# Weight halves stored even columns first, read by TensorE as pairs 2 KB apart

## The chip, the cores and the metric

The kernel runs on one core of a Trainium2 chip. The metric is the device time of one execution in microseconds (us). The core has TensorE (PE, its weight loads are shown apart as PEld), VectorE (DVE), ScalarE (ACT), GpSimd (POOL) and SyncE (SP), which issues the loads.

## The reference

Two transformer-like blocks run one after the other on 256 tokens of width 2048, in float32. Cut to the matmuls, which matter here:

```python
# first block
h = rmsnorm(x);  proj = h @ w_in                 # 2048 -> 8192
y = concat(hgrn2_mixer(...), short_conv_mixer(...))   # mixer: small per-head products
x = x + y @ w_out
g, u = split(rmsnorm(x) @ w_gate_up);  x = x + (silu(g) * u) @ w_down
x = rmsnorm(x)
# second block
ada = silu(c) @ w_ada + b_ada                     # a vector times 2048 x 12288
proj = (rms(x) * (1 + sc1) + sh1) @ w_in          # 2048 -> 8256
y_a = mla_attention(...);  y_b = stick_breaking(...)  # 8 heads each, 256 tokens
x = x + gt1 * ((sig(gl_a) * (y_a @ w_mla) + sig(gl_b) * (y_b @ w_sb)) @ w_out)
g, u = split((rms(x) * (1 + sc2) + sh2) @ w_ffn_in);  x = x + gt2 * ((silu(g) * u) @ w_ffn_out)
```

With 256 tokens every weight is used once, and all of them (some 580 MB in float32) are streamed from device memory.

## The kernel before

A weight matrix comes in units of 512 rows by 512 columns: 1 MB, in SBUF as `raw` [128 partitions, 4, 512], one transfer each, four buffers in turn. A unit is worked in two chunks of two 128-row slices (`kt`). Float32 accuracy is had by splitting: for each chunk ACT casts `raw` to the rounded format float32r, `whi` [128, 2, 512] (L870 in `cast`), and DVE takes `wlo = raw - whi` (L1262 in `low`). The activations lie split in the same way, as stationary operands (`hH`/`hL`, `mH`/`mL`, `aH`/`aL` and others).

`products(v)` in `tensor_program` does a visit: for each of the two slices and each of the two halves of the tokens (`m`) three matmuls of 128 x 128 stationary by 512 moving columns into one PSUM bank: activation high by weight high (L839), high by low (L840), low by high (L841). So a chunk has 12 of them, each reading 512 adjacent float32r columns of `whi` or `wlo`. One block, `kpe`, has its weights as the stationary operand instead (L821 to L823, 48 matmuls of 256 columns).

The order is written out in `Plan`: blocks, chunks, visits, and for each visit which chunk is split then, three chunks ahead of its use (four buffers of `whi` and `wlo`, four more at two boundaries between stages). Between the visits stand the small pieces of the mixers, the attention, the norms and the transposes (L553), each under a semaphore. `w_ada` is multiplied on DVE from its own `raw` units (L1689). Some of the small pieces read their operands through patterns with steps. The one that the prediction uses is `pair_ap`, with which `hgrn` reads `Qx` as the moving operand of L633 on TensorE (plain float32; 8 matmuls a level, each shown as 2 passes of 128 columns) and `Kx` in the copies L1056 and L1061 on ACT:

```python
        def pair_ap(t, base, n, h):                                  # L502
            ap = t[:, :, :]
            return bass.AP(tensor=ap.tensor, offset=ap.offset + base,
                           ap=[list(ap.ap[0]), [2 * h, n // (2 * h)], [1024 + h, 2], [1, h]])
```

It reads `h` neighbours, then `h` neighbours 1024 + h elements on, and so by turns. The first level has h = 1: single elements, 4100 bytes apart. It doubles from level to level, up to 64. On DVE `carry` (L1667) goes through the same tensors in runs of h out of 2h elements, for h = 1 single elements at a step of 2, and L1635 reads both its inputs at a step of 2 elements; L1615 has its inputs in order.

Of the kernel before, what the change touches and what calls it, by code (L numbers as in the profile page):

```python
# [15 lines left out]
ALU = mybir.AluOpType  # L16
# [6 lines left out]
RAW = 4  # L23
# [233 lines left out]
class Counts:  # L257
# [13 lines left out]
    def ev(self, name, *key):  # L271
        self.n[name] = self.n.get(name, 0) + 1
        if not self.real:
            assert (name,) + key not in self.value, (name, key)
            self.value[(name,) + key] = self.n[name]
        return self.of(name), 1

    def on(self, name, *key):
        if not self.real:
            return self.of(name), 1  # L280
        return self.of(name), self.value[(name,) + key]
# [5 lines left out]
def two_block_kernel(nc, a, out):  # L287
    ctx = ExitStack()
    with ctx:
# [6 lines left out]
        ev, on = bk.ev, bk.on  # L296
# [11 lines left out]
        def take(n):  # L308
            o = top[0]
            top[0] += n + (-n) % 64  # L310
            return o

        def new(name, shape, dt=F32):
            return at(name, shape, dt, take(nbytes(shape)))

        raw = [new(f"raw{i}", [P, 4, 512]) for i in range(RAW)]
        whi = [new(f"whi{i}", [P, 2, 512], F32R) for i in range(HL)]
        wlo = [new(f"wlo{i}", [P, 2, 512], F32R) for i in range(HL)]
# [11 lines left out]
        kpe = new("kpe", [P, 2, 64])  # L330
# [5 lines left out]
        for i in range(7):  # L336
            o = take(2 * KB)
# [74 lines left out]
        def visit(v):  # L412

            return sem_visit, v + 1

        def acc(b, m):

            return banks[2 * (b.index % 2) + m]
# [25 lines left out]
        def side_read(*key):  # L444

            n = bk.bank.get(key, 0) if not bk.real else bk.bank[key]
            return sem_side[n % 4], n // 4 + 1

        def raw_here(u):

            return sem_raw[u % RAW], 16 * (u // RAW + 1)
# [38 lines left out]
        def f(ap):  # L490
            return ap.bitcast(F32)
# [10 lines left out]
        def pair_ap(t, base, n, h):  # L502
            ap = t[:, :, :]
            return bass.AP(tensor=ap.tensor, offset=ap.offset + base,
                           ap=[list(ap.ap[0]), [2 * h, n // (2 * h)], [1024 + h, 2], [1, h]])

        def ev_tmp(b, m):
            return T[2 * (b.index % 2) + m]

# [41 lines left out]
        def tensor_program(e):  # L551
# [3 lines left out]
            def turn_tokens(b, m, key):  # L555

                t, o = ev_tmp(b, m), next_bank(e, *key)
                for k in range(4):
                    ins = turn(o[:, P * k:P * k + P], t[:, P * k:P * k + P])
                ins.then_inc(*ev("pe_turn", *key))  # L560
# [201 lines left out]
            def amid(v):  # L762

                for w, v0 in enumerate(SK):
                    k = v - v0
                    if k == 7:
                        norm_first(w, 0, 2)
                        norm_first(w, 0, 3)
                    elif k in (11, 12):
                        norm_first(w, 1, 2 * (k - 11))  # L770
                        norm_first(w, 1, 2 * (k - 11) + 1)
                    elif 14 <= k <= 17:
                        norm_rest(w, 2 + (k - 14) // 2, (k - 14) % 2)

            def left_here(b, i, ci, m):
# [28 lines left out]
                elif b.kind == "out2" and b.arg == (0,) and i == 0 and m == 0 and kt % 4 == 0:  # L804
                    e.wait_ge(*side_read(pl.at["sb", kt // 4].index, 0))
                    e.wait_ge(*side_read(pl.at["sb", kt // 4].index, 1))

            def products(v):
                c, ms, _ = pl.visits[v]
                b, ci, u, hf = pl.chunks[c]  # L810
                wh, wl, (xh, xl) = whi[pl.buf[c]], wlo[pl.buf[c]], halves[b.lhs]
                if ms[0] == 0:
                    e.wait_ge(*on("dve_lo", c, 0))
                if b.kind == "kpe":
                    wh = wh[:, :, :].rearrange("p a b -> p (a b)").rearrange("p (k n) -> p k n", k=KT)
                    wl = wl[:, :, :].rearrange("p a b -> p (a b)").rearrange("p (k n) -> p k n", k=KT)
                    o = acc(b, 0)[0:64, 0:S]
                    if pl.acc_n[b.index, 0]:
                        e.wait_ge(sem_acc[2 * (b.index % 2)], pl.acc_n[b.index, 0])
                    for kt in range(KT):  # L820
                        e.matmul(o, wh[:, kt, :], xh[:, kt, :], start=kt == 0, stop=False)  # L821
                        e.matmul(o, wl[:, kt, :], xh[:, kt, :], start=False, stop=False)
                        ins = e.matmul(o, wh[:, kt, :], xl[:, kt, :], start=False, stop=kt == KT - 1)  # L823
                    ins.then_inc(*ev("visit", v))
                    return
                n = len(b.kts)
                for i in range(2):
                    k = 2 * ci + i
                    kt = b.kts[k]
                    if i == 1:  # L830
                        amid(v)
                        if c == 0:
                            e.wait_ge(*on("dve_lo", 0, 1))
                    for m in ms:
                        left_here(b, i, ci, m)
                        if k == 0 and pl.acc_n[b.index, m]:
                            e.wait_ge(sem_acc[2 * (b.index % 2) + m], pl.acc_n[b.index, m])
                        o, sl = acc(b, m)[:, :], slice(P * m, P * m + P)
                        e.matmul(o, xh[:, kt, sl], wh[:, i, :], start=k == 0, stop=False)  # L839
                        e.matmul(o, xh[:, kt, sl], wl[:, i, :], start=False, stop=False)  # L840
                        ins = e.matmul(o, xl[:, kt, sl], wh[:, i, :], start=False, stop=k == n - 1)  # L841
                ins.then_inc(*ev("visit", v))

            e.wait_ge(*on("dve_ones"))
# [8 lines left out]
        def scalar_program(e):  # L853
            def cast(c):

                b, ci, u, hf = pl.chunks[c]
                i = pl.buf[c]
                if pl.after[c] is not None:
                    e.wait_ge(*visit(pl.after[c]))
                if c == 0:  # L860
                    for k in range(2):
                        e.wait_ge(sem_first[k], 16)
                        e.copy(whi[i][:, k:k + 1, :], raw[0][:, k:k + 1, :]).then_inc(*ev("act_hi", c, k))
                        feature(1 + k)
                    return
                if c == 2:
                    e.wait_ge(sem_first[2], 16)
                else:
                    e.wait_ge(*raw_here(u))
                e.copy(whi[i][:, :, :], raw[u % RAW][:, 2 * hf:2 * hf + 2, :]).then_inc(*ev("act_hi", c, 0))  # L870

            def feature(kt):

                if kt in XT_AT:
                    e.wait_ge(sem_xT[XT_AT.index(kt)], 16)
                e.activation(hH[:, kt, :], xT[:, kt, :], ACT.Copy, bias=0.0, scale=vc("attn_norm_w", kt)).then_inc(
                    *ev("act_h1", kt))
# [371 lines left out]
        def vector_program(e):  # L1249
            def low(c):  # L1250

                b, ci, u, hf = pl.chunks[c]
                i = pl.buf[c]
                if c == 0:
                    for k in range(2):
                        e.wait_ge(*on("act_hi", 0, k))
                        e.tensor_tensor(wlo[i][:, k:k + 1, :], raw[0][:, k:k + 1, :], f(whi[i][:, k:k + 1, :]),
                                        ALU.subtract).then_inc(*ev("dve_lo", 0, k))
                        feature(1 + k)
                    return  # L1260
                e.wait_ge(*on("act_hi", c, 0))
                e.tensor_tensor(wlo[i][:, :, :], raw[u % RAW][:, 2 * hf:2 * hf + 2, :], f(whi[i][:, :, :]),  # L1262
                                ALU.subtract).then_inc(*ev("dve_lo", c, 0))

            def feature(kt):

                e.wait_ge(*on("act_h1", kt))
                e.scalar_tensor_tensor(hL[:, kt, :], xT[:, kt, :], vc("attn_norm_w", kt), f(hH[:, kt, :]), ALU.mult,
                                       ALU.subtract).then_inc(*ev("dve_h1", kt))
# [755 lines left out]
        for program in (tensor_program, scalar_program, vector_program, gpsimd_program, sync_program):  # L2025
            program(Dry())
        bk.again()
        with nc.Block() as block:

            @block.tensor  # L2030
            def _(e):
                tensor_program(e)

            @block.scalar
            def _(e):
                scalar_program(e)

            @block.vector
            def _(e):
                vector_program(e)  # L2040

            @block.gpsimd
            def _(e):
                gpsimd_program(e)

            @block.sync
            def _(e):
                sync_program(e)
# [88 lines left out]
```

## Time and profile before

| | us |
|---|---|
| Time, median of 3 runs | 2601.33 (2598.67 to 2601.68) |
| The profiled execution's own time | 2601.2 |
| Its span in the profile | 2599.4 |
| PE busy | 2588.7 |
| DVE busy | 1757.9 |
| ACT busy | 1197.9 |
| POOL busy | 27.1 |

The span runs from the first to the last instruction of the profiled execution. A matmul's busy time in the profile is from its start to its modelled end and overlaps the next one's; how fast matmuls follow one another is read from their starts. The loads move 582.37 MB, 224 GB/s over the span.

### The profile page before, as it was taken

To read this page: it belongs to the slowest core of one execution; us is meant where nothing else is said; L and a number is where in the kernel's file an instruction comes from. 1 tells how busy PE (TensorE), PEld (TensorE's weight loads), DVE (VectorE), ACT (ScalarE), POOL (GpSimd) and SP (SyncE) were. 2 spreads that over 40 slices of the span, in tenths; PEclk is the share of its full clock that TensorE was granted. 3 is DMA by queue.
4 is the path that set the end of the run, shared out by engine and by line. 5 is a ranking of instruction groups with operands and counts; after the bars stand their busy time and mean duration, and the time that the engine had idled before them with its cause. 6 is when DMAs were issued, how large, how long until landed. Compare 5 with 4: busy or idle time off the path is not lost.

```text
span 2599.4 us, 29559 instructions
## 1 busy us (share of the span) xinstructions
PE 2588.7 (100%) x11904; PEld 2152.7 (83%) x11904; DVE 1757.9 (68%) x2158; ACT 1197.9 (46%) x1465; POOL 27.1 (1%) x27
## 2 busy tenths in 40 slices
PE   9999999999999999999999999999999999999999
PEld 8888888888888888888788888888788888888887
DVE  5787788778777778776565464466677755555554
ACT  6444444444443344445655454444544443344443
POOL 0000000000000000000000000000000000000000
PEclk9999999999999999999999999999999999999999
DMA  8656656788788888786454445555577755555554
GB/s 320 225 183 222 212 204 233 248 301 290 272 289 284 289 286 287 281 289 228 144 178 164 148 163 186 192 183 178 178 275 284 268 181 195 192 191 195 182 193 144
DMA packets 82631, 582.37 MB, mean 224 GB/s; under 512 B 9408, under 2 KB 9792, under 8 KB 12608
## 3 DMA queue, kind: packets, MB, share of 16 engines
q1 hardware_dynamic: 82352, 580.38, 63.6%
q8 instruction: 94, 1.54, 0.2%
q14 instruction: 41, 0.34, 0.0%
q10 hardware_dynamic: 144, 0.12, 0.0%
HBM read 578.36 MB, written 2.10 MB: 223 GB/s over the span
## 4 chain that ended last, share of the span: by engine, by line
PE 97%; DVE 1%; DMA 1%; issue 0%; SPq 0%; ACT 0%; POOL 0%; POOLq 0%; ACTq 0%
PE bank L839 31%; PE bank L841 31%; PE bank L840 31%; PE bank L553 2%; PE bank L633 1%; DMA raw<-in_w_in_dram 1%; PE bank L671 0%; DVE wlo L1262 0%; PE bank L682 0%; PE bank L683 0%; PE bank L652 0%; PE bank L641 0%; PE bank L651 0%; PE bank L672 0%; PE bank L694 0%
## 5 line engine op out<-in xcount | busy, mean ns | idle before, releaser
L1262 DVE TENSOR_TENSOR wlo<-raw,whi 128x1024 fp32r<-128x1024 f32 x886 | 1082.1, 1223 | 728.8 <-ACT whi L870 720.2
L870 ACT CAST whi<-raw 128x1024 fp32r<-128x1024 f32 x886 | 932.8, 1054 | 1009.1 <-PE bank L841 995.5
L839 PE MATMUL bank<-whi,hH 128*128 128x512 f32 x2528 | 997.4, 395 | 0.5 <-DVE wlo L1262 0.4
L841 PE MATMUL bank<-whi,hL 128*128 128x512 f32 x2528 | 985.5, 390 | 0.0
L840 PE MATMUL bank<-wlo,hH 128*128 128x512 f32 x2528 | 984.7, 390 | 0.0
L841 PEld LDWEIGHTS bank<-whi,hL 128*128 128x128 f32 x2528 | 474.8, 188 | 99.9
L839 PEld LDWEIGHTS bank<-whi,hH 128*128 128x128 f32 x2528 | 475.2, 188 | 97.6 <-DVE wlo L1262 1.4
L840 PEld LDWEIGHTS bank<-wlo,hH 128*128 128x128 f32 x2528 | 475.4, 188 | 95.6
L839 PE MATMUL bank<-whi,aH 128*128 128x512 f32 x704 | 274.5, 390 | 0.0
L1689 DVE SCALAR_TENSOR_TENSOR adacc<-raw,stat,adacc 128x512 f32<-128x512 f32 x360 | 269.7, 749 | 6.8
L841 PE MATMUL bank<-whi,aL 128*128 128x512 f32 x704 | 274.0, 389 | 0.0
L840 PE MATMUL bank<-wlo,aH 128*128 128x512 f32 x704 | 273.9, 389 | 0.0
L840 PEld LDWEIGHTS bank<-wlo,aH 128*128 128x128 f32 x704 | 132.2, 188 | 27.3
L841 PEld LDWEIGHTS bank<-whi,aL 128*128 128x128 f32 x704 | 132.2, 188 | 27.3
L839 PEld LDWEIGHTS bank<-whi,aH 128*128 128x128 f32 x704 | 132.2, 188 | 27.2
L553 PEld LDWEIGHTS bank<-ident,tmp 128*128 128x128 f32 x530 | 63.4, 141 | 17.6 <-DVE tmp L1813 4.1
L553 PE MATMUL bank<-ident,tmp 128*128 128x128 f32 x530 | 73.9, 274 | 3.4 <-DVE tmp L1813 2.8
L839 PE MATMUL bank<-whi,mH 128*128 128x512 f32 x128 | 50.6, 395 | 0.0
L841 PE MATMUL bank<-whi,mL 128*128 128x512 f32 x128 | 50.0, 390 | 0.0
L840 PE MATMUL bank<-wlo,mH 128*128 128x512 f32 x128 | 49.8, 389 | 0.0
L945 ACT CAST aH<-bank 128x512 fp32r<-128x512 f32 x44 | 23.6, 590 | 45.7 <-PE bank L553 45.7
L1938 POOL TENSOR_TENSOR stat<-stat 128x4 f32<-128x4 f32 (+2 forms) x22 | 25.1, 1150 | 1823.0 <-DVE stat L1282 1061.9
(295 smaller groups left out, 1423.9 us busy)
## 6 DMA issues: line engine op xcount, KB each, us to landing
raw<-in_w_gu_dram SPq DMA_DIRECT2D x176, 1024.0 KB, 4.9
raw<-in_w_ada_dram SPq DMA_DIRECT2D x96, 1024.0 KB, 4.9
raw<-in_w_down_dram SPq DMA_DIRECT2D x88, 1024.0 KB, 4.8
raw<-in_w_in_dram SPq DMA_DIRECT2D x62, 1024.0 KB, 4.8
raw<-in_w_in2b_dram SPq DMA_DIRECT2D x56, 1024.0 KB, 4.8
raw<-in_w_out_dram SPq DMA_DIRECT2D x32, 1024.0 KB, 4.8
raw<-in_w_in2a_dram SPq DMA_DIRECT2D x8, 1024.0 KB, 5.0
raw<-in_w_mla_dram SPq DMA_DIRECT2D x8, 1024.0 KB, 4.7
```

Source lines behind the costliest of these rows:

```text
L553: return e.transpose(o, i, ident[0:n, 0:n])
L633: ins = e.matmul(o[:, P * hd:P * hd + P], KC[:, base:base + P], qq, start=True, stop=True)
L839: e.matmul(o, xh[:, kt, sl], wh[:, i, :], start=k == 0, stop=False)
L840: e.matmul(o, xh[:, kt, sl], wl[:, i, :], start=False, stop=False)
L841: ins = e.matmul(o, xl[:, kt, sl], wh[:, i, :], start=False, stop=k == n - 1)
L870: e.copy(whi[i][:, :, :], raw[u % RAW][:, 2 * hf:2 * hf + 2, :]).then_inc(*ev("act_hi", c, 0))
L945: e.copy(aH[:, k0:k0 + 4, P * m:P * m + P], v4(side(b.index, m))).then_inc(*ev("act_half", b.index, m))
L1262: e.tensor_tensor(wlo[i][:, :, :], raw[u % RAW][:, 2 * hf:2 * hf + 2, :], f(whi[i][:, :, :]), ALU.subtract).then_inc(*ev("dve_lo", c, 0))
L1689: ins = e.scalar_tensor_tensor(d, src, col, d, ALU.mult, ALU.add)
L1938: e.tensor_tensor(sc(o, n), sc(i, n), sc(b_half, n), ALU.pow).then_inc(*ev("pool_pow", *key))
```

## The change

`whi` and `wlo` keep their size and place, but within a chunk the columns are stored in another order: first the even columns of both slices (2 x 256 elements), then the odd columns of both. The cast on ACT and the subtraction on DVE read `raw` at a step of 2 elements and write in order. The matmuls read the 512 columns of a slice as 256 pairs, the second of a pair 512 elements (2048 bytes) behind the first, so that the columns reach the array, and PSUM, in their old order. The `kpe` block stays as it was.

```diff
+        def as_loaded(t, k, n):
+            return t[:, k:k + n, :].rearrange("p k (a b) -> p b k a", b=2)
+
+        def parted(t, k, n):
+            return t[:, :, :].rearrange("p b (k a) -> p b k a", k=2)[:, :, k:k + n, :]
...
+            def woven(w, i):
+                ap = w[:, :, :]
+                return bass.AP(tensor=ap.tensor, offset=ap.offset + 256 * i, ap=[list(ap.ap[0]), [1, 256], [512, 2]])
...
-                        e.matmul(o, xh[:, kt, sl], wh[:, i, :], start=k == 0, stop=False)
-                        e.matmul(o, xh[:, kt, sl], wl[:, i, :], start=False, stop=False)
-                        ins = e.matmul(o, xl[:, kt, sl], wh[:, i, :], start=False, stop=k == n - 1)
+                        e.matmul(o, xh[:, kt, sl], woven(wh, i), start=k == 0, stop=False)
+                        e.matmul(o, xh[:, kt, sl], woven(wl, i), start=False, stop=False)
+                        ins = e.matmul(o, xl[:, kt, sl], woven(wh, i), start=False, stop=k == n - 1)
...
-                        e.copy(whi[i][:, k:k + 1, :], raw[0][:, k:k + 1, :]).then_inc(*ev("act_hi", c, k))
+                        e.copy(parted(whi[i], k, 1), as_loaded(raw[0], k, 1)).then_inc(*ev("act_hi", c, k))
...
-                e.copy(whi[i][:, :, :], raw[u % RAW][:, 2 * hf:2 * hf + 2, :]).then_inc(*ev("act_hi", c, 0))
+                if b.kind == "kpe":
+                    e.copy(whi[i][:, :, :], raw[u % RAW][:, 0:2, :]).then_inc(*ev("act_hi", c, 0))
+                else:
+                    e.copy(parted(whi[i], 0, 2), as_loaded(raw[u % RAW], 2 * hf, 2)).then_inc(*ev("act_hi", c, 0))
...
-                e.tensor_tensor(wlo[i][:, :, :], raw[u % RAW][:, 2 * hf:2 * hf + 2, :], f(whi[i][:, :, :]),
-                                ALU.subtract).then_inc(*ev("dve_lo", c, 0))
+                if b.kind == "kpe":
+                    ...
+                else:
+                    e.tensor_tensor(parted(wlo[i], 0, 2), as_loaded(raw[u % RAW], 2 * hf, 2), f(parted(whi[i], 0, 2)),
+                                    ALU.subtract).then_inc(*ev("dve_lo", c, 0))
```

## Rows read from the trace of the kernel before

**Rows 1.** The page: busy time, share, instructions; the clock in 40 slices.

```profile
PE 2588.7 (100%) x11904; PEld 2152.7 (83%) x11904; DVE 1757.9 (68%) x2158; ACT 1197.9 (46%) x1465; POOL 27.1 (1%) x27
...
PEclk9999999999999999999999999999999999999999
```

**Rows 2.** The page: the chain that ended last, by engine and by line.

```profile
PE 97%; DVE 1%; DMA 1%; issue 0%; SPq 0%; ACT 0%; POOL 0%; POOLq 0%; ACTq 0%
PE bank L839 31%; PE bank L841 31%; PE bank L840 31%; PE bank L553 2%; PE bank L633 1%; DMA raw<-in_w_in_dram 1%; PE bank L671 0%; DVE wlo L1262 0%; PE bank L682 0%; PE bank L683 0%; PE bank L652 0%; PE bank L641 0%; PE bank L651 0%; PE bank L672 0%; PE bank L694 0%
```

**Rows 3.** Costliest groups: count, busy us, mean ns, idle before, releaser.

```profile
L1262 DVE TENSOR_TENSOR wlo<-raw,whi 128x1024 fp32r<-128x1024 f32 x886 | 1082.1, 1223 | 728.8 <-ACT whi L870 720.2
L870 ACT CAST whi<-raw 128x1024 fp32r<-128x1024 f32 x886 | 932.8, 1054 | 1009.1 <-PE bank L841 995.5
```

**Rows 4.** Groups by form on PE: line L839, all its left-hand operands.

```profile
L839 PE MATMUL bank<-whi,hH 128*128 128x512 f32 x2528 | 997.4, 395 | 0.5 <-DVE wlo L1262 0.4
...
L839 PE MATMUL bank<-whi,aH 128*128 128x512 f32 x704 | 274.5, 390 | 0.0
...
L839 PE MATMUL bank<-whi,mH 128*128 128x512 f32 x128 | 50.6, 395 | 0.0
...
L839 PE MATMUL bank<-whi,yaH 128*128 128x512 f32 x64 | 25.5, 398 | 0.0
...
L839 PE MATMUL bank<-whi,ybH 128*128 128x512 f32 x64 | 24.9, 389 | 0.0
...
L839 PE MATMUL bank<-xhi,hH 128*128 128x512 f32 x32 | 14.0, 438 | 1.7 <-DVE hL L1822 1.7
...
L839 PE MATMUL bank<-whi,ckH 128*128 128x512 f32 x32 | 12.7, 396 | 0.0
...
L839 PE MATMUL bank<-whi,cqH 128*128 128x512 f32 x24 | 9.3, 389 | 0.0
```

**Rows 5.** Timeline of PE near 300 us: start, duration (us), what.

```profile
299.74 0.39 PE L841 MATMUL bank<-whi,hL 128*128 128x512 f32 x1
...
303.82 0.39 PE L841 MATMUL bank<-whi,hL 128*128 128x512 f32 x1
```

**Rows 6.** Timeline near the start: consecutive matmuls on PE.

```profile
8.55 0.63 PE L841 MATMUL bank<-whi,hL 128*128 128x512 f32 x1
...
8.98 0.63 PE L839 MATMUL bank<-whi,hH 128*128 128x512 f32 x1
...
9.40 0.63 PE L840 MATMUL bank<-wlo,hH 128*128 128x512 f32 x1
```

**Rows 7.** Chain in order of time: Qx in order, h = 1, h = 2.

```profile
102.81 1.78 PE bank L633 x16
112.77 2.66 PE bank L633 x16
123.61 1.92 PE bank L633 x16
```

**Rows 8.** Single lines (min/median/max ns), then DVE groups by form.

```profile
L1056 ACT COPY KC<-Kx x2: 1542/1548/1555, 106.1 to 307.5; 128x1024 f32<-128x1024 f32 x2
...
L1061 ACT COPY KC<-Kx x12: 1045/1056/1218, 115.5 to 367.7; 128x1024 f32<-128x1024 f32 x12
...
L1667 DVE TENSOR_TENSOR Kx<-Kx,TA x16: 676/685/687, 112.3 to 378.0; 128x512 f32<-128x512 f32 x16
...
L1615 DVE TENSOR_TENSOR Qx<-qT,TA 128x1024 f32<-128x1024 f32 x4 | 4.9, 1218 | 0.0
...
L1635 DVE TENSOR_TENSOR TB<-TA 128x1024 f32<-128x1024 f32 x2 | 2.4, 1207 | 0.0
```

**Rows 9.** Who waited for whom: us in total, times, longest us.

```profile
ACT whi L870 <- PE bank L841: 995.5, 658, 3.5
...
DVE wlo L1262 <- ACT whi L870: 720.2, 505, 4.1
```

**Rows 10.** Timeline of PE: the last matmul.

```profile
2595.14 0.39 PE L841 MATMUL bank<-whi,aL 128*128 128x512 f32 x1
```

More of the change, by code:

```diff
@@ L1256, in low @@
                         e.wait_ge(*on("act_hi", 0, k))
-                        e.tensor_tensor(wlo[i][:, k:k + 1, :], raw[0][:, k:k + 1, :], f(whi[i][:, k:k + 1, :]),
+                        e.tensor_tensor(parted(wlo[i], k, 1), as_loaded(raw[0], k, 1), f(parted(whi[i], k, 1)),
                                         ALU.subtract).then_inc(*ev("dve_lo", 0, k))
@@ L1261, in low @@
                 e.wait_ge(*on("act_hi", c, 0))
-                e.tensor_tensor(wlo[i][:, :, :], raw[u % RAW][:, 2 * hf:2 * hf + 2, :], f(whi[i][:, :, :]),
-                                ALU.subtract).then_inc(*ev("dve_lo", c, 0))
+                if b.kind == "kpe":
+                    e.tensor_tensor(wlo[i][:, :, :], raw[u % RAW][:, 0:2, :], f(whi[i][:, :, :]), ALU.subtract).then_inc(
+                        *ev("dve_lo", c, 0))
+                else:
+                    e.tensor_tensor(parted(wlo[i], 0, 2), as_loaded(raw[u % RAW], 2 * hf, 2), f(parted(whi[i], 0, 2)),
+                                    ALU.subtract).then_inc(*ev("dve_lo", c, 0))
             def feature(kt):
```

## The prediction

> **What bounds the kernel now.** I read the busy times first, then the chain of waits, then single matmuls in the timeline. The engines' busy times give PE 2588.7 us of a span of 2599.4 us, at a clock slice of 9 (the top digit) in all 40 slices; DVE is at 68%, ACT at 46% [rows 1]. The chain that ended last is PE for 97%, and three lines make 93% of it: the products of a weight half with a left-hand half (L839 to L841) [rows 2]. DVE and ACT are idle before the splitting of the weights and wait, in the end, for those matmuls: ACT 995.5 us in 658 waits, DVE behind ACT 720.2 us [rows 3, 9]. So the time is the number of 512-column matmuls times their pace.
>
> The count, by left-hand halves, is 2528 + 704 + 128 + 64 + 64 + 32 + 32 + 24 = 3576 for L839, and L840 and L841 have as many: 10,728 [rows 4]. The busy figure of a row (390 ns each) is a latency and overlaps the next one; the pace is the distance of the starts: 299.74 to 303.82 in 18 steps, 226.7 ns [rows 5]. 10,728 x 226.7 ns = 2432 us. The remaining 167 us of the span are the first loads, the transposes, the small matmuls and the last block's epilogue.
>
> **A look at the pace.** 512 columns in 226.7 ns are 0.443 ns a column; a column per cycle of 2.4 GHz would be 0.417 ns, 213.3 ns in all. At the start, while the duration is still 0.63 us, the same matmuls start 0.43 and 0.42 us apart [rows 6], which is 512 columns at 1.2 GHz (426.7 ns) with nothing lost. The loss of 13 ns exists at the fast clock alone. I read it so: at 2.4 GHz the moving operand (4 bytes a column) asks for just more than its read path delivers. An operand that is harder to read will then show in the pace at once; nothing lies above it as cover.
>
> **Part 1: TensorE's reads (on the path).** Each of the 10,728 matmuls now reads its 512 columns as 256 pairs; within a pair the addresses are 2048 bytes apart, the next pair is 4 bytes on. No 512-column matmul of before reads so, but two instructions do something close. The copy L1056 on ACT and the first level of L633 on PE read through pair_ap with h = 1: element, element 4100 bytes on, back to 8 bytes behind the first.
> - PE: a stretch of 16 passes of 128 fp32 columns takes 1.78 us where the operand lies in order (or in long runs), 2.66 us at h = 1, 1.92 us at h = 2, where two neighbours are read before each jump [rows 7]. That is 111.25, 166.25 and 120 ns a pass. Less the 4.6 ns by which 111.25 exceeds 128 columns at 1.2 a ns (106.7), h = 1 costs 161.6 / 128 = 1.263 ns an element against 0.833.
> - ACT: the copy of 1024 elements takes 1548 ns at h = 1, median 1056 ns at the other levels (1218 at most) [rows 8]. Taking 0.833 ns for an element in order, h = 1 costs 0.833 + 492/1024 = 1.31 ns an element.
>
> Two engines with different work come to nearly one absolute figure, 1.26 to 1.31 ns for each read that goes to another place than the one before. The series on PE speaks for a limit rather than a surcharge: with 4, 2 and 1 neighbours between moves the loss for each move is nothing for slow fp32 reading in order, (120 - 111.25)/64 = 0.14 ns at h = 2, 0.43 ns at h = 1. It grows as less work lies between moves. In the woven read there is one element of 0.417 ns between moves, so the limit itself sets the pace: 512 x 1.263 + 4.6 = 651 ns. Bounds: below, 213 ns (a column per cycle, all loss gone); above, twice 0.833 ns for each read, 853 ns plus 5, as if each read occupied its port for two slots of the slow fp32 row. I take 651, by the PE row, which is the same engine, the same shape of access and the nearest distance; only the number format's rate differs.
> 10,728 x (651 - 226.7) ns = +4552 us.
>
> The Trainium skill, Advanced Engine Details and Errata, section Memory Cachelines, says that SBUF is read in lines of 16 bytes, that at least two hits on a line are needed to hide its latency, and that another line for each access costs a penalty, for which it gives no figure. The traces of h = 1 and h = 2 agree in kind [rows 7, 8]. By this rule too the casts below (two hits a line) stay free and the woven matmul (one hit, then away) is slow.
>
> **Part 2: ACT's cast (off the path).** 894 casts of 1024 elements (and two of 512) read raw with a step of 8 bytes and write in order. Bounds: 1054 ns as now [rows 3], 1548 ns as the copy whose every read is elsewhere [rows 8]. I take 1.06 to 1.22 us. What hides it: ACT's waits for PE, and at 651 ns a chunk of 12 matmuls lasts 7.8 us rather than 2.7. Even the upper bound adds 0.49 x 894 = 442 us to 1198 busy, in a much longer run.
>
> **Part 3: DVE's subtraction (off the path).** The same read of raw. DVE has such steps already: L1635 reads both inputs at a step of 2 elements, 1207 ns for 1024; L1615 reads in order, 1218 ns; L1667 reads and writes at a step of 2 at its first level and lies within 676 to 687 ns at all levels that read TA, the first among them [rows 8]. So 1223 ns stays, cost nothing. Were it 1.3 ns an element (+0.3 us), DVE would go to 2000 us busy, still cover.
>
> **Part 4: the rest.** No instruction, wait, semaphore or transfer is added or moved; kpe's block (48 matmuls), transposes and attention products are as they were. Slower chunks free raw later, so transfers spread out and hide better. The end (two DVE operations and the store, behind a last matmul that starts 4.3 us before the span's end [rows 10]) stays.
>
> **Sum.** The profiled execution took 2601.2 us (span 2599.4), within 0.2 us of the median 2601.33. 2601 + 4552 = 7153; I say 7150 us. Its own range goes from 1.22 to 1.32 ns an element: 6920 to 7460.
>
> **Rivals.**
> - *A surcharge, not a limit* (20%). Each move adds what h = 1 added, 55 ns for 128 elements, so 220 for 512: 447 ns. Nearly the same comes of one element per slot of 0.833 ns (427 ns). For it: the additive reading fits two of the rows as well. Against: the growing series above. 2601 + 10,728 x 0.220 = 4960 us (4750 with 427).
 Against: nothing shows two addresses in one slot. 2601 + 10,728 x 0.1017 = 3690 us.
> - *A harder conflict* (6%). Distances of exactly 2048 bytes meet in the same part of the memory: 858 ns, 9370 us. Against: 4100 bytes is nearly a power of two as well and cost 1.26.
> - *The clock falls* (3%). With the array waiting for operands the granted clock may go to its lower level, 1.2 GHz. The woven matmuls don't feel it (427 ns is under 651), the other 167 us at most double: 7320 us.
> - *No effect* (7%). The queue ahead of the array absorbs the pattern or reads whole lines of both places. Against: h = 1 slowed PE at half this appetite. 2601 us. The Trainium skill, TensorE: Matmul & The Clock Gate, section Step-by-step: what each phase is for, calls throughput "purely `N cycles`", whatever the operand's layout; by that rule nothing changes. The h = 1 row contradicts it in this trace.
> - *Faster* (3%). The loss of 13.4 ns a matmul that the fast clock alone shows comes from neighbouring reads meeting each other, and places 2 KB apart don't meet: 213.3 ns, 2601 - 10,728 x 0.0134 = 2457 us. It decides only if two distant reads cost less than 0.887 ns together; the h = 1 row has 2.5 ns. A gain has no more room than this, since a column per cycle is the floor.
>
> **How the numbers follow.** The forecast has 47%, the rivals as given. The range must hold 8 in 10: forecast, surcharge and pair make 81%, and the clock's case lies inside, so 3600 to 7500 us; the likeliest's own range is 6920 to 7460. A change under 0.2% (5 us) couldn't be told from none. Slower by more: 47 + 20 + 14 + 6 + 3 = 90%; same 7%; faster 3%.
>
> **What the profile after would show.** Right: starts of L839 to L841 about 0.65 us apart; L839 to L841 still over 90% of the chain; ACT's cast under 1.25 us and DVE's subtraction at 1.22; traffic near 582 MB / 7.15 ms = 81 GB/s; DVE at about 25% of the span. A pace of 0.45 or 0.33 us names the surcharge or the pair. Wrong altogether: starts at 0.227 us. If a cast took over 2 us, or DVE or ACT came into the chain, part 2 or 3 would be wrong. If the slices of PEclk fell to 5, the clock's case is there.

## The result, and the profile after

The changed kernel takes 2494.63 us (median of 4 runs, 2493.96 to 2495.91) against 2600.32 us before; the ratio is 0.9594, with a 95% interval of 0.9578 to 0.9611. Forecast was 7150 us, with 3 in 100 for a gain. The sign was wrong, and so was the range.

The page of the changed kernel: span, busy times, the clock in 40 slices, and the chain that ended last, by engine and by line. L852, L853 and L854 are now the three matmul lines [before: rows 2], L886 the cast, L1282 the subtraction.

```profile
span 2493.5 us, 29559 instructions
...
PE 2474.2 (99%) x11904; PEld 2169.3 (87%) x11904; DVE 1984.0 (80%) x2158; ACT 1675.0 (67%) x1465; POOL 31.7 (1%) x27
...
PEclk9999999999999999999999999999999999999999
...
PE 93%; DVE 3%; ACT 2%; issue 1%; DMA 1%; SPq 0%; POOL 0%; POOLq 0%; ACTq 0%
PE bank L852 29%; PE bank L853 29%; PE bank L854 29%; PE bank L561 2%; DVE wlo L1282 1%; PE bank L641 1%; ACT whi L886 1%; DMA raw<-in_w_in_dram 1%; DVE xlo L1282 0%; PE bank L679 0%; POOL stat L1958 0%; PE bank L690 0%; PE bank L691 0%; DMA raw<-in_w_in2a_dram 0%; DVE hL L1842 0%
```

The instruction count is the same, and so is the clock: its top digit in all 40 slices [rows 1]. PE is busy for less time, DVE and ACT for more [rows 1], and DVE and ACT have entered the chain, which was 97% PE [rows 2]. Two things have changed, in opposite directions.

First the pace. The timeline of PE near 1000 us (start, duration in us):

```profile
999.70 0.38 PE L853 MATMUL bank<-wlo,hH 128*128 128x512 f32 x1
...
1002.94 0.38 PE L853 MATMUL bank<-wlo,hH 128*128 128x512 f32 x1
```

That is 15 steps of 216 ns, against 226.7 [rows 5]. Over the last 53 to 55 steps of each profile, 12 us, I get 226.6 ns before and 215.8 after. 10,728 x 10.8 ns = 116 us, which is more than the whole gain in span (2599.4 - 2493.5 = 105.9 us). The Trainium skill, TensorE: Matmul & The Clock Gate, section Wait — 56ns, not 53.3ns?, gives 215.7 ns for 512 columns back to back at the fast clock; the changed kernel is at that figure, the kernel before was not.

Second, the splitting of the weights. Costliest groups of the changed kernel (count, busy us, mean ns, idle before, releaser):

```profile
L886 ACT CAST whi<-raw 128x1024 fp32r<-128x1024 f32 x885 | 1408.6, 1599 | 543.1 <-PE bank L854 455.3
L1282 DVE TENSOR_TENSOR wlo<-raw,whi 128x1024 fp32r<-128x1024 f32 x885 | 1323.1, 1503 | 457.2 <-ACT whi L886 455.8
```

The cast went from 1054 to 1599 ns, the subtraction from 1223 to 1503 [rows 3]. ACT's wait for PE has shrunk from 995.5 to 455.3 us [rows 9]: the cover was used. Where it isn't enough, at the boundary between the two blocks, the chain shows it (changed kernel, in order of time; `xlo` is one of the additional buffers there, used like `wlo`):

```profile
1166.39 1.47 DVE xlo L1282
1167.86 1.48 DVE wlo L1282
1169.33 1.48 DVE xlo L1282
```

There the chain runs through subtractions back to back. 116 gained on PE less 106 in the span leaves some 10 us lost. This boundary is only a small part of it. `host_order`, a version further below, has the new pace without the slow splitting, and can be set beside the changed kernel matmul by matmul. The changed kernel's matmul at 1165.06 us starts 2.8 us later than its partner there, the one at 1172.10 us 3.8 us later: 1 us for this boundary. The lag is 7.2 us at 1290 us, 9.3 at 1730, 11.0 at 1780 and 12.2 from 2010 us to the end. So the loss is made up in several places, with 1 to 3 us in each.

### The profile page after: what moved, and what is told of

Its sections match the earlier page's. It is cut to its first block, busy times and chain, and to the rows that moved or that the text cites. A ratio compares the mean times of both kernels' runs of the same rounds, so it can differ in the third digit from the quotient of the medians.

```text
span 2493.5 us, 29559 instructions
## 1 busy us (share of the span) xinstructions
PE 2474.2 (99%) x11904; PEld 2169.3 (87%) x11904; DVE 1984.0 (80%) x2158; ACT 1675.0 (67%) x1465; POOL 31.7 (1%) x27
## 4 chain that ended last, share of the span: by engine, by line
PE 93%; DVE 3%; ACT 2%; issue 1%; DMA 1%; SPq 0%; POOL 0%; POOLq 0%; ACTq 0%
PE bank L852 29%; PE bank L853 29%; PE bank L854 29%; PE bank L561 2%; DVE wlo L1282 1%; PE bank L641 1%; ACT whi L886 1%; DMA raw<-in_w_in_dram 1%; DVE xlo L1282 0%; PE bank L679 0%; POOL stat L1958 0%; PE bank L690 0%; PE bank L691 0%; DMA raw<-in_w_in2a_dram 0%; DVE hL L1842 0%
## 5 line engine op out<-in xcount | busy, mean ns | idle before, releaser
L886 ACT CAST whi<-raw 128x1024 fp32r<-128x1024 f32 x885 | 1408.6, 1599 | 543.1 <-PE bank L854 455.3
L1282 DVE TENSOR_TENSOR wlo<-raw,whi 128x1024 fp32r<-128x1024 f32 x885 | 1323.1, 1503 | 457.2 <-ACT whi L886 455.8
L852 PE MATMUL bank<-whi,hH 128*128 128x512 f32 x2528 | 972.2, 385 | 1.9 <-DVE wlo L1282 1.3
L853 PE MATMUL bank<-wlo,hH 128*128 128x512 f32 x2528 | 959.4, 379 | 0.0
L854 PE MATMUL bank<-whi,hL 128*128 128x512 f32 x2528 | 959.2, 379 | 0.0
L852 PEld LDWEIGHTS bank<-whi,hH 128*128 128x128 f32 x2528 | 478.9, 189 | 70.5 <-DVE wlo L1282 3.9
L854 PEld LDWEIGHTS bank<-whi,hL 128*128 128x128 f32 x2528 | 478.7, 189 | 67.7
L853 PEld LDWEIGHTS bank<-wlo,hH 128*128 128x128 f32 x2528 | 479.0, 189 | 64.9
L852 PE MATMUL bank<-whi,aH 128*128 128x512 f32 x704 | 267.6, 380 | 0.8 <-DVE wlo L1282 0.8
L853 PE MATMUL bank<-wlo,aH 128*128 128x512 f32 x704 | 266.9, 379 | 0.0
L854 PE MATMUL bank<-whi,aL 128*128 128x512 f32 x704 | 266.9, 379 | 0.0
L852 PEld LDWEIGHTS bank<-whi,aH 128*128 128x128 f32 x704 | 133.2, 189 | 19.9 <-DVE wlo L1282 1.2
L854 PEld LDWEIGHTS bank<-whi,aL 128*128 128x128 f32 x704 | 133.1, 189 | 18.8
L853 PEld LDWEIGHTS bank<-wlo,aH 128*128 128x128 f32 x704 | 133.2, 189 | 18.5
L852 PE MATMUL bank<-whi,mH 128*128 128x512 f32 x128 | 49.2, 384 | 0.0
L853 PE MATMUL bank<-wlo,mH 128*128 128x512 f32 x128 | 48.5, 379 | 0.0
L854 PE MATMUL bank<-whi,mL 128*128 128x512 f32 x128 | 48.5, 379 | 0.0
```

The source lines that it names most:

```text
L852: e.matmul(o, xh[:, kt, sl], woven(wh, i), start=k == 0, stop=False)
L853: e.matmul(o, xh[:, kt, sl], woven(wl, i), start=False, stop=False)
L854: ins = e.matmul(o, xl[:, kt, sl], woven(wh, i), start=False, stop=k == n - 1)
L886: e.copy(parted(whi[i], 0, 2), as_loaded(raw[u % RAW], 2 * hf, 2)).then_inc(*ev("act_hi", c, 0))
L1282: e.tensor_tensor(parted(wlo[i], 0, 2), as_loaded(raw[u % RAW], 2 * hf, 2), f(parted(whi[i], 0, 2)), ALU.subtract).then_inc(*ev("dve_lo", ...
```

## The experiments

There are four questions: is it the reading or the storage that makes the pace; which property of the pattern; what happened to the casts; and can the loss be avoided.

### Reading alone, storing alone

`read_only2` leaves the casts as before and changes the matmuls' pattern; `store_only2` has the new casts and matmuls that read in order. In both, TensorE also waits for the second slice before the very first chunk, because there a read of one slice touches both; this happens once.

```diff
 # read_only2, against before
-  e.matmul(o, xh[:, kt, sl], wh[:, i, :], ...)
+  e.matmul(o, xh[:, kt, sl], woven(wh, i), ...)       # [1, 256], [512, 2] from 256 * i; the other two alike
 # store_only2, against after
-  e.matmul(o, xh[:, kt, sl], woven(wh, i), ...)
+  e.matmul(o, xh[:, kt, sl], wh[:, i, :], ...)        # the other two alike
```

> Stored as before (casts read and write in order), TensorE reads pairs 2 KB apart; the columns reach PSUM in another order, so the result is another. In the very first chunk TensorE waits for both slices. Theory E (even- and odd-numbered columns of a float32r operand are fetched as two streams, each quick while it stays in a 16-byte line for four reads): pace 216 ns, casts 1055 and subtractions 1223 ns, about 2482 us. Rival B (the new storage order, what ACT and DVE write and when, eases TensorE's reads): 226.7 ns, 2600 us. Rival C (TensorE's reads in pairs are what slows the casts in the changed kernel): 216 ns, but casts near 1600 and subtractions near 1500 ns, 2495 us.

> Stored even columns first, with the casts at a step of 8 bytes, TensorE reads 512 columns in order (the columns reach PSUM in another order, so the result is another). Theory E: pace 226.7 ns; casts 1600 and subtractions 1500 ns if the step of 8 bytes alone is their price, time 2600 to 2612 us. Rival B (storage eases TensorE's reads): 216 ns, 2495 us. Rival C: casts 1055 to 1120 ns, 2600 us.

`read_only2`: 2483.34 us, ratio 0.955 (0.9534 to 0.9566). `store_only2`: 2600.47 us, ratio 1.0008 (0.9998 to 1.0017), no difference that can be told. Groups of `read_only2`, then of `store_only2`:

```profile
L1267 DVE TENSOR_TENSOR wlo<-raw,whi 128x1024 fp32r<-128x1024 f32 x886 | 1080.5, 1222 | 633.1 <-ACT whi L875 628.4
...
L845 PE MATMUL bank<-wlo,hH 128*128 128x512 f32 x2528 | 958.6, 379 | 0.0
L875 ACT CAST whi<-raw 128x1024 fp32r<-128x1024 f32 x886 | 927.9, 1049 | 917.0 <-PE bank L846 897.8
```

```profile
L1282 DVE TENSOR_TENSOR wlo<-raw,whi 128x1024 fp32r<-128x1024 f32 x885 | 1081.6, 1223 | 733.7 <-ACT whi L886 725.7
...
L886 ACT CAST whi<-raw 128x1024 fp32r<-128x1024 f32 x885 | 991.1, 1121 | 963.6 <-PE bank L854 955.8
...
L853 PE MATMUL bank<-wlo,hH 128*128 128x512 f32 x2528 | 984.9, 390 | 0.0
```

The reading makes the pace (a duration of 379 ns goes with 216 between starts, 390 with 227); the storage has no part in it. But the casts are slow only when both parts are there: 1121 ns with the step of 8 bytes alone, 1049 with the pairs alone, 1599 with both. The subtraction goes the same way: 1223, 1222 and 1503 ns. My rival C was half right: the pairs slow the casts, but only those that go at a step.

### Which property of the pattern

`sweep` and `sweep2` store as before and give each chunk's 12 matmuls another pattern in rotation, each on a line of its own, so that all stand in one profile. Both leave the casts in order.

```diff
+  if q == 2:                                          # pairs 16 B apart; q = c % 15
+      ins = e.matmul(o, x_, rd(w_, 0, 512, [8, 64], [1, 4], [4, 2]), ...)
+  if q == 10:                                         # runs of two, 1 KB apart
+      ins = e.matmul(o, x_, rd(w_, 0, 512, [2, 128], [256, 2], [1, 2]), ...)
```

> Stored as before; the matmuls' read pattern changes from chunk to chunk in a round of 15 (the result is another). Theory A (neighbour reads of a pair meet in one 16-byte line): 226.7 ns for the reads in order and for pairs 8 B apart, 216 ns for pairs 16, 32, 64, 256 B, 1 KB, 2 KB and 2052 B apart and for four places 512 B apart; runs of two 226.7. Rival D (the pair has to lie in different larger parts of the memory): 216 ns only from some larger distance on. Rival E (each line of 16 bytes must be entered less often, a buffer for each of two streams): step 8 B in order slower than 226.7 ns. For the pattern of L633's first level (step 8 B in pairs 2052 B apart) my prediction's limit of 1.26 ns an element gives 651 ns; if it is the step of 8 bytes rather than the jump that costs, all three patterns with that step are slow and the pairs 2 KB apart are not.

> Stored as before; the matmuls' read pattern changes from chunk to chunk in a round of 11, five of them in plain float32 (the result is another). Theory E (two streams, even- and odd-numbered columns, each with its own last line of 16 bytes): each element twice 216 ns, the same four elements 216, pairs 1 KB apart begun within a line 216, step 8 B in pairs 2 KB apart 227 (two reads a line and stream), two of each four elements near 470 as the plain step of 8 bytes in the first sweep (one read a line and stream). Theory A (the two reads of a pair collide if they are in one line): each element twice and the same four 227, two of each four 227. Plain float32, if it has one stream (per pass of 512 columns): in order 427 ns, pairs 2 KB apart and the pattern of L633's first level about 650, runs of two and step 8 B about 460. If plain float32 has two streams as well: pairs 2 KB apart 427.

Timeline of `sweep`: the first and the twelfth matmul of a chunk in order (L817), with pairs 8 B apart (L820), pairs 16 B apart (L823), at a step of 8 bytes (L853), and with the pattern of L633's first level (L859).

```profile
1003.54 0.62 PE L853 MATMUL bank<-whi,hH 128*128 128x512 f32 x1
...
1008.49 0.63 PE L853 MATMUL bank<-whi,hL 128*128 128x512 f32 x1
...
1011.68 0.39 PE L859 MATMUL bank<-whi,hH 128*128 128x512 f32 x1
...
1014.18 0.39 PE L859 MATMUL bank<-whi,hL 128*128 128x512 f32 x1
1014.40 0.39 PE L817 MATMUL bank<-whi,hH 128*128 128x512 f32 x1
...
1016.90 0.39 PE L817 MATMUL bank<-whi,hL 128*128 128x512 f32 x1
1017.12 0.39 PE L820 MATMUL bank<-whi,hH 128*128 128x512 f32 x1
...
1019.62 0.39 PE L820 MATMUL bank<-whi,hL 128*128 128x512 f32 x1
1019.85 0.38 PE L823 MATMUL bank<-whi,hH 128*128 128x512 f32 x1
...
1022.22 0.38 PE L823 MATMUL bank<-whi,hL 128*128 128x512 f32 x1
```

Divide each difference by 11. In ns between starts: in order 227; pairs 8 B apart 227; pairs 16 B apart 215.5; pairs 32, 64 and 256 B, 1 KB and 2052 B apart 216; step 8 B 450; step 8 B in pairs, 2 KB or 2052 B apart, 227 to 229; and from the same view four places 512 B apart 281, runs of two 1 KB apart 333, runs of four 251. (2 KB apart: 223 in a chunk that begins behind other work, the same 379 ns duration as the rest.)

So the pattern that my forecast was built on, h = 1, costs a float32r matmul 227 ns, exactly what reading in order costs it. And 16 bytes of distance are enough, so rival D (larger parts of the memory) is out. Theory A (neighbours collide) gave all the pairs rightly, but missed the four places (216 expected, 281 measured) and the runs of two (226.7 expected, 333 measured).

`sweep2` separates theory A from theory E. The first and the twelfth matmul with each element read twice (L820) and with two of each four elements (L823); then chunks in plain float32 in order (L835, two passes each), in pairs 2 KB apart (L838) and with the pattern h = 1 (L844):

```profile
1018.58 0.38 PE L820 MATMUL bank<-whi,mH 128*128 128x512 f32 x1
...
1020.96 0.38 PE L820 MATMUL bank<-whi,mL 128*128 128x512 f32 x1
1021.17 0.62 PE L823 MATMUL bank<-whi,mH 128*128 128x512 f32 x1
...
1026.12 0.63 PE L823 MATMUL bank<-whi,mL 128*128 128x512 f32 x1
...
1034.96 1.02 PE L835 MATMUL bank<-whi,mH 128*128 128x512 f32 x2
...
1044.41 1.02 PE L835 MATMUL bank<-whi,mL 128*128 128x512 f32 x2
...
1045.70 1.24 PE L838 MATMUL bank<-whi,mH 128*128 128x512 f32 x2
...
1057.58 1.24 PE L838 MATMUL bank<-whi,mL 128*128 128x512 f32 x2
...
1069.46 1.47 PE L844 MATMUL bank<-whi,mH 128*128 128x512 f32 x2
...
1083.83 1.48 PE L844 MATMUL bank<-whi,mL 128*128 128x512 f32 x2
```

Each element twice: 216 ns. Both reads of a pair fall on one address there, so theory A, which expected 227, is refuted. Two of each four: 450 ns, though the whole sequence (0, 1, 4, 5, 8, 9) enters new 16 bytes only with every second read. What counts is what every second column sees: 0, 4, 8, a new 16 bytes each time. With pairs 8 B apart (0, 2, 1, 3, 4, 6, 5, 7) it sees 0, 1, 4, 5, two reads to each 16 bytes, and a matmul takes 227 ns. Theory E stands: all of these patterns behave as if a float32r operand were fetched as two streams, the even-numbered and the odd-numbered columns.

The numbers agree too. Plain float32, per pass of 512 (half the distance of two starts, since each matmul has two passes): in order 430, step 8 B 450, runs of two 454, pairs 2 KB apart 540, h = 1 653 ns. Take the time per element of one stream (float32r: pace / 256; plain: pass / 512):

| what one stream sees | plain float32, ns | float32r, ns (pattern) |
|---|---|---|
| step of 4 B | 0.84 (in order) | 0.84 (pairs) |
| step of 8 B | 0.88 (step 8 B) | 0.89 (in order) |
| two places by turns, step 4 B | 1.05 (pairs 2 KB apart) | 1.10 (four places) |
| two places by turns, step 8 B | 1.28 (h = 1) | 1.30 (runs of two) |
| step of 16 B | not measured | 1.76 (step 8 B) |

Reading in order in float32r is, for each stream, a walk at 8 bytes, and pays 0.04 to 0.05 ns an element, as plain float32 does at a step of 8 bytes. The change makes it a walk at 4 bytes. My expectation of 650 ns for plain pairs 2 KB apart missed (540): not each jump is dear, but each 16 bytes newly entered without a second read on them at once. h = 1 enters new ones in half of its reads, pairs in a quarter, the step of 16 B in all; by the table's differences that is about 0.9 ns for each in all three. One pattern isn't covered by this: runs of four (251 ns, 0.98 for an element of a stream) have two reads to each 16 bytes at once and still cost 0.09 ns more than reading in order.

### The casts

`cast_order` and `cast_pairs` rotate seven patterns of cast and subtraction, the first with TensorE in order, the second with pairs 2 KB apart.

```diff
+  if q == 1:                                          # read step 8 B; q = c % 7
+      e.copy(walk(whi[i], 0, [1, 1024]), walk(raw[u % RAW], 1024 * hf, [1, 2], [512, 2], [2, 256]))
+  if q == 3:                                          # read pairs 2 KB apart
+      e.copy(walk(whi[i], 0, [1, 1024]), walk(raw[u % RAW], 1024 * hf, [1, 512], [512, 2]))
```

> TensorE reads in order; the cast and the subtraction change their pattern from chunk to chunk in a round of 7 (each chunk's weights end up in some order, so the result is another). If a step of 8 bytes costs by itself: ACT 1055 in order, 1600 for the step of 8 bytes, 1550 for pairs 2 KB apart, 1200 for runs of two, 1600 or more for a step of 16 bytes, DVE 1223 in order and 1500 for the step of 8 bytes. If it is a collision with TensorE's fetches, the same patterns cost less in the run in which TensorE fetches in pairs. The write side: if writes are buffered, writing at a step costs nothing (1055 and 1223).

> The cast and the subtraction change their pattern from chunk to chunk in the same round of 7 as in the run cast_order, but TensorE reads pairs 2 KB apart throughout (pace 216 ns; the result is another). If the casts' price is their own: the same durations as with TensorE in order, within 20 ns. If the price comes from a collision with TensorE's fetches of lines: lower than there for every pattern that is slow, since each stream of TensorE then opens a line every 8 columns instead of every 4.

Groups of `cast_order`: ACT reading at a step of 16 B (L887), pairs 2 KB apart (L883), step 8 B (L879), in order (L877).

```profile
L887 ACT CAST whi<-raw 128x1024 fp32r<-128x1024 f32 x127 | 258.4, 2035 | 141.2 <-PE bank L846 141.2
...
L883 ACT CAST whi<-raw 128x1024 fp32r<-128x1024 f32 x127 | 165.8, 1306 | 50.6 <-PE bank L846 48.0 <-DMA raw<-in_w_gu_dram 2.0
...
L879 ACT CAST whi<-raw 128x1024 fp32r<-128x1024 f32 x127 | 142.8, 1124 | 136.7 <-PE bank L846 136.4 <-DMA raw<-in_w_in_dram 0.3
...
L877 ACT CAST whi<-raw 128x1024 fp32r<-128x1024 f32 x127 | 134.0, 1055 | 131.7 <-PE bank L846 125.7 <-DMA raw<-in_w_gu_dram 6.0
```

The same four in `cast_pairs` (L892, L888, L884, L882):

```profile
L892 ACT CAST whi<-raw 128x1024 fp32r<-128x1024 f32 x127 | 369.2, 2907 | 120.2 <-PE bank L851 82.9 <-DMA raw<-in_w_gu_dram 27.1 <-DMA raw<-in_w_down_dram 10.0
...
L884 ACT CAST whi<-raw 128x1024 fp32r<-128x1024 f32 x127 | 197.1, 1552 | 106.6 <-PE bank L851 77.1 <-DMA raw<-in_w_gu_dram 19.7 <-DMA raw<-in_w_down_dram 9.9
...
L888 ACT CAST whi<-raw 128x1024 fp32r<-128x1024 f32 x127 | 163.8, 1290 | 63.5 <-PE bank L851 30.4 <-DMA raw<-in_w_gu_dram 23.1 <-DMA raw<-in_w_down_dram 9.6
...
L882 ACT CAST whi<-raw 128x1024 fp32r<-128x1024 f32 x127 | 133.2, 1050 | 51.2 <-PE bank L851 34.7 <-DMA raw<-in_w_gu_dram 14.9 <-DMA raw<-in_w_down_dram 1.5
```

It is a collision, since the same instruction takes 1124 or 1552 ns by what TensorE does; and it goes the other way from what I had expected: TensorE's pairs make it worse. Only steps suffer (8 B: +428 ns, 16 B: +872, and writing at 8 B: 1130 to 1535); in order, runs of two (1100 and 1099) and pairs don't. Pairs have a price of their own beside either pattern of TensorE, 1306 and 1290 ns, less than the 1550 I expected. Writing pairs 2 KB apart costs 2.06 to 2.07 us either way: writes aren't free, contrary to what I had supposed. DVE goes with ACT: the step of 8 B 1222 and 1496 ns.

The small pieces of the changed kernel say the same. The first level of `carry` on `Qx` goes at a step of 8 bytes: its two operations take 1.29 us together in the kernel before (from 117.36 us on), and 1.73 us in the changed one, where TensorE reads pairs beside them (from 112.99 us on). The copy on ACT with h = 1 isn't slowed by the pairs: 1548 ns before, 1554 after. It moves by 8 bytes as well, but in two places by turns.

`collide` keeps the casts at the step of 8 B and changes TensorE's pattern every 20 chunks.

```diff
 # against sweep, which has the same function trio; the casts are those of the changed kernel
-  ins = trio(c % 15, ...)
+  ins = trio(c // 20 % 6, ...)    # in order; pairs 16 B, 64 B, 1 KB, 2 KB apart; each element twice
```

> Casts and subtractions at the step of 8 bytes as in the changed kernel; TensorE's pattern changes every 20 chunks in a round of 6 (in order, pairs 16 B, 64 B, 1 KB and 2 KB apart, each element twice; the result is another). If it is the distance of the pair that makes the casts slow (two places of the memory busy at once): ACT 1121 in order and for each element twice, up to 1600 for pairs, rising or appearing with the distance. If it is TensorE's higher pace (216 against 227 ns, all five other patterns): 1550 to 1600 for all but in order. DVE by the same rule 1223 or 1500.

Its casts during pairs 2 KB apart (L915), each element twice (L917), pairs 1 KB apart (L913), in order (L907), pairs 16 B (L909) and 64 B apart (L911):

```profile
L915 ACT CAST whi<-raw 128x1024 fp32r<-128x1024 f32 x140 | 225.1, 1611 | 83.2 <-PE bank L837 65.3 <-DMA raw<-in_w_gu_dram 11.6 <-PE bank L834 5.8
L917 ACT CAST whi<-raw 128x1024 fp32r<-128x1024 f32 x140 | 222.0, 1593 | 86.2 <-PE bank L840 66.3 <-PE bank L837 11.3 <-DMA raw<-in_w_gu_dram 8.2
L913 ACT CAST whi<-raw 128x1024 fp32r<-128x1024 f32 x135 | 212.7, 1580 | 96.9 <-PE bank L834 73.9 <-PE bank L831 14.7 <-DMA raw<-in_w_gu_dram 8.1
...
L907 ACT CAST whi<-raw 128x1024 fp32r<-128x1024 f32 x161 | 183.6, 1142 | 142.1 <-PE bank L825 122.7 <-PE bank L840 9.6 <-DMA raw<-in_w_in_dram 5.0
L909 ACT CAST whi<-raw 128x1024 fp32r<-128x1024 f32 x156 | 175.4, 1127 | 157.9 <-PE bank L828 131.8 <-PE bank L825 17.6 <-DMA raw<-in_w_down_dram 8.4
L911 ACT CAST whi<-raw 128x1024 fp32r<-128x1024 f32 x153 | 174.7, 1143 | 165.3 <-PE bank L831 148.5 <-PE bank L828 16.6
```

TensorE's matmuls have a median of 379 ns in all five patterns other than in order, so its pace is not the cause; and each element twice is slow without any distance, so it is not two places at once either. Both my expectations fail. What the three slow patterns share, and the two quick ones lack, is that each stream of TensorE walks word by word through unbroken stretches of 256 elements; in the quick pairs it skips every second 16 or 64 bytes, and in order it goes at 8 bytes. That is only a description. Why it meets a step of 8 bytes on another engine stays open.

### Two versions without the loss

`host_order` lays the weights out in device memory with each 512 columns even ones first; nothing is at a step in SBUF, and the pairs are 1 KB apart. `weave8` leaves device memory alone and parts the columns within each 8.

```diff
 # host_order, in layout(): for all units but w_ada
+  u.reshape(-1, P, 4, 256, 2).transpose(0, 1, 2, 4, 3)
 #             and woven: [1, 256], [256, 2] from 512 * i
 # weave8: cast and subtraction read raw as
+  [8, 64 * n], [1, 2], [2, 4]
 #         and woven: [8, 64], [1, 4], [4, 2] from 512 * i
```

> The weights are laid out in device memory even columns first within each 512 columns, so the loads bring them in that order, casts and subtractions read and write in order, and TensorE reads pairs 1 KB apart; same result as before. Theory A: pace 216 ns and casts 1055, subtractions 1223 ns: 2485 us, some 10 us better than the changed kernel, whose ACT and DVE come late at the boundaries. Rival D (1 KB is not enough): 226.7 ns, 2600 us. Rival C: casts near 1600 ns, 2495 us.

> The even and the odd columns lie apart by lines only: in each 8 columns first the four even ones, then the four odd ones. Casts and subtractions read 0, 2, 4, 6, 1, 3, 5, 7 of each 8 and write in order; TensorE reads pairs 16 B apart; same result as before. Theory E gives TensorE four reads to a line and stream: 216 ns a matmul. For the casts: if, as with the step of 8 bytes in the changed kernel, every access that opens a line each second read collides with TensorE's pairs, 1550 to 1600 ns and 1500 ns, and 2490 to 2496 us; if only newly opened lines count (here one in four reads, as in order), near 1055 to 1100 and 1223 ns, and 2482 us.

`host_order`: 2481.19 us, ratio 0.9545 (0.9529 to 0.9561). `weave8`: 2483.83 us, ratio 0.9555 (0.9539 to 0.9571). Both are below the changed kernel's 0.9594 (0.9578 to 0.9611), with intervals that don't touch; the two can't be told from each other. `weave8`'s cast and subtraction:

```profile
L1274 DVE TENSOR_TENSOR wlo<-raw,whi 128x1024 fp32r<-128x1024 f32 x886 | 1080.4, 1222 | 644.3 <-ACT whi L881 642.5
L881 ACT CAST whi<-raw 128x1024 fp32r<-128x1024 f32 x886 | 1015.9, 1148 | 854.3 <-PE bank L851 814.5
```

The cast is at 1148 ns, above the 1055 to 1100 expected but off the path again. `host_order`'s span of 2481.3 us is 118.1 under that of before: the 116 us of the pace in full (where the other 2 us come from is open). Going by the ratios, the changed kernel is 10 to 13 us behind `weave8`, `read_only2` and `host_order`. These three have the same pace and quick splitting, so its loss is the slow splitting.

## Why the prediction was wrong, point by point

- *What bounds the kernel* was right: PE's 10,728 matmuls and their pace. That 13 ns a matmul were lost at the fast clock alone, in the reading, was right, and with it that a gain had at most that much room; 10.8 of the 13.4 came back. The explanation beside it was wrong: not the 4 bytes a column are too much for the read path, since pairs ask for as many and take 216 ns. So the conclusion that any operand harder to read shows at once had no ground.
- *Part 1 failed*, at "I take 651, by the PE row, which is the same engine, the same shape of access and the nearest distance; only the number format's rate differs". The format doesn't only differ in rate: it is fetched as two streams, and a pair's two halves go to different ones. The h = 1 row was plain float32, one stream [rows 7]. Its pattern in float32r costs 227 ns, and the pattern of the change 216 where I had put 651; the term 10,728 x (651 - 226.7) = +4552 us came out as -116 us. The second fault is the reading "for each read that goes to another place than the one before": plain pairs 2 KB apart cost 1.05 ns an element, not 1.26. h = 1 steps by 8 bytes in each place and enters new lines twice as often.
- *ACT and PE agreeing* on 1.26 to 1.31 ns was real for these two rows (plain float32 with h = 1 gave PE 1.28 again in `sweep2`); I took agreement between them for validity in a third case that neither showed.
- *The rival "the pair is the unit"* had the two fetches side by side, the right mechanism, but priced it with the price of h = 1 (1.263 ns) and so came to 3690 us. With the price of a slow read in order, 0.833 ns (the one slot of 1.2 GHz that it speaks of), it would have come to 256 x 0.833 = 213 ns, near the measured 216.
- *The rival "faster"* named the right sign and nearly the right size, 2457 us against 2495, with a wrong mechanism (neighbours that collide); each element twice refutes that. Had it been the forecast, its hit would have been luck.
- *The rivals "surcharge", "harder conflict", "no effect" and "the clock falls"* are ruled out by the starts (216 ns, not 447, 858 or 226.7) and by a clock that stayed at its top digit in all 40 slices.
- *Part 2 and 3* (casts at most 1.22 us, subtraction 1223 ns) were wrong in size: 1599 and 1503, the cast even above its upper bound of 1548. The rows used were right for TensorE reading in order (1121 and 1223 in `store_only2`), not for TensorE in pairs; L1635 and L1667 stood in the right place but beside a TensorE that read no pairs. That they were covered was right but for some 10 us, because the cover (2.6 us a chunk, not 7.8) was that of a fast PE.
- The rule on lines of 16 bytes (Advanced Engine Details and Errata, Memory Cachelines, of the Trainium skill) is borne out, nearly: two hits a line at a step of 8 bytes cost 0.04 ns an element of a stream, one costs 0.9, and two that don't follow each other (h = 1) cost 0.44. What I applied wrongly is whose hits are counted: each stream's own, not the operand's.

## What to carry to other kernels

A float32r moving operand read in order loses 5% of TensorE's rate at the fast clock (226.7 against 215.8 ns for 512 columns). Read it in pairs at least 16 bytes apart, so that even and odd columns each walk through adjacent words, and store the columns so. Two ways cost nothing that these runs can see: lay the weights out so in device memory, which leaves the work to whoever prepares them, or part the columns within each 8 in the cast, with pairs 16 bytes apart. What to avoid is a cast at a step of 8 bytes beside pairs 1 or 2 KB apart. Before using a row as a price, ask whether it has the same format and the same neighbours in time: here the same instruction took 1121 or 1599 ns by what another engine read.

## What the runs showed of the hardware that I had not expected

- Moving operands in float32r behave as two streams, of the even and the odd columns (table above); h = 1 and reading in order cost the same 227 ns.
- ACT and DVE at a step of 8 bytes are slowed by 0.27 to 0.47 ns an element while TensorE reads in pairs 1 or 2 KB apart or each element twice (1124 to 1552, 1222 to 1496, 1121 to 1599 ns), not while it reads in order or in pairs 16 or 64 bytes apart.
- Beside a TensorE that reads in order, a cast that writes pairs 2 KB apart takes 2073 ns, 1018 more than one in order (1055); one that reads them so takes 1306, only 251 more.
